# Combining two expert outputs per token: rows of 64 tokens of both choices stacked in the 128 partitions, one matmul in half of the output columns

## The chip, the cores and the metric

One core of one Trainium2 chip runs the whole program. The metric is the device time of one launch in microseconds (us). The kernel before takes 2280.2 us, the median of three runs (2276.58 to 2281.41). All arithmetic is in 32-bit floating point.

## What is computed

The program is one inference step of a decoder layer: RMSNorm, a combined projection, sliding-window attention and a gated delta rule side by side, an output projection, then a mixture of experts in which each token picks two of 64 experts, and a final RMSNorm. It handles 2048 prompt tokens and 64 sample tokens. The change touches only the last step, cut here to what matters:

```python
# hierarchical_moe / reference: two experts per token, gates w0 and w1
y = w0[:, None] * expert_out[first choice] + w1[:, None] * expert_out[second choice]
h = h + y                                  # h: the residual, (tokens, 1024)
out = h * rsqrt(mean(h * h, axis=-1) + 1e-6) * norm_final
```

## The kernel before

The last phase is the function `moe`. Its expert part runs 64 blocks and a few overflow blocks, each with 128 token places: the weights of one expert (3 MB) are loaded by SyncE (SP) into a ring of four buffers in `w_arena`, TensorE (PE) does the three projections (lines 3221 and 3230), and GpSimd (POOL) writes the block's rows to a table `S["y"]` in DRAM with an indirect transfer (line 2911). That table has 2 x 2176 rows of 1024 values: row `t*128 + p` holds the first choice of token p of tile t, the row 2176 further the second choice.

When the last block's rows are in DRAM, ScalarE (ACT) raises `experts_stored`, and the combining stage begins. It runs over 17 tiles: 16 of 128 prompt tokens and one (t = 16) of the 64 sample tokens. `w_arena`, free by now, holds 8 buffers `pair[c]` (two rows of 1024 values a partition, CB = 8) and 8 buffers `out[o]` (OB = 8). Tile by tile:

- **SP**, `fetch(t)`, line 2832: one transfer of 1 MB puts both rows of token p into partition p of `pair[t % 8]`. Eight fetches are issued at the start; `fetch(t + 8)` waits for `weighted` of tile t.
- **ACT**, `weights(t)`, line 3015: two diagonal 128x128 matrices, the identity scaled by the gate of either choice, into `diag`.
- **PE**, `weigh(t)`, line 3260: for each half of the 1024 columns, the first choice's diagonal times the first rows, then the second's added in the same PSUM bank. That is 4 matmuls of 128x512; in 32-bit each is two instructions, so 8 instructions a tile. A tile takes two of the eight PSUM banks, so `weigh(t)` waits for `summed` of tile t - 4.
- **VectorE (DVE)**, `add(t)`, line 3176: PSUM plus the residual `h_all` into `out[t % 8]`. From tile 8 on it waits until the store of tile t - 8 has landed.
- **ACT**, line 3029: the square, with its sum over the row. **POOL**, `root(t)`, lines 2960 and 2962: the power -0.5.
- **DVE**, `scale(t)`, line 3182: the product with the root and the gain. DVE's order is written out: `scale(t - BEHIND)` follows `add(t)`, with BEHIND = 4.
- **SP**, `store(t)`, line 2842: 512 KB to the output. SP's order is written out too: for each t, `fetch(t + 8)`, then `store(t - BEHIND)`.

All of SP's transfers share one queue (q1). Two earlier places of SP are named by the prediction. Line 400 stores the sample tokens' projections from 64 partitions to DRAM; for the table `s_qkv` both sides have 64 rows outermost, and for the table `s_conv_s` the DRAM side is written as 8 sequences x 8 rows, so its outermost dimension has 8 entries while the side in SBUF has 64 partitions. Line 1442 copies caches from DRAM to DRAM; the copies from `in_cache_swa_k` and `in_cache_swa_v` have an outermost dimension of 8 on both sides. Lines 2459 (attention) and 964 (sample projection) are matmuls of 128 rows by 64 output columns that alternate between the output partitions 0 to 63 and 64 to 127.

Of the kernel before, what the change touches and what calls it, by code (L numbers as in the profile page):

```python
# [12 lines left out]
ALU = mybir.AluOpType  # L13
ACT = mybir.ActivationFunctionType
AX = mybir.AxisListType.X

P = 128
D = 1024
# [8 lines left out]
HD = 64  # L27
# [20 lines left out]
HOMES = TILES * P  # L48
# [2611 lines left out]
def moe(nc, A, S, O, K):  # L2660
    T, E = TILES, EPG
# [7 lines left out]
    with Phase(nc, "p5_") as ctx:  # L2669
        sb, sem = ctx.sb, ctx.sem  # L2670
        on = Once(ctx)
# [8 lines left out]
        two = range(2)  # L2680
# [3 lines left out]
        y_arena = sb("y_arena", [P, 6 * DE])  # L2684
        h_all = sb("h_all", [P, T, D])

        def cut(arena, at, shape):
            size = math.prod(shape)
            ap = arena[:, at:at + size]
            if len(shape) == 2:  # L2690
                return ap.rearrange("p (a b) -> p a b", a=shape[0])
            if len(shape) == 3:
                return ap.rearrange("p (a b c) -> p a b c", a=shape[0], b=shape[1])
            return ap
# [6 lines left out]
        y = [cut(y_rows, b * D, (D,)) for b in two]  # L2701
# [2 lines left out]
        midt = [cut(y_arena, (4 + b) * DE, (FC, P)) for b in two]  # L2704

        CB, OB = 8, 8
        BEHIND = 4
        kept = range(BEHIND + 1)
        pair = [cut(w_arena, 2 * c * D, (2, D)) for c in range(CB)]
        ya = [[pair[c][:, k, :] for c in range(CB)] for k in range(2)]  # L2710
        out = [cut(w_arena, (2 * CB + c) * D, (D,)) for c in range(OB)]

        n3 = LAST[1] - LAST[0]
        ident, w = K["ident"], K["w"]
# [28 lines left out]
        spare = sb("spare", [P, 3])  # L2743
        home = [sb(f"home{b}", [P, 1], I32) for b in two]
        gain = cut(y_arena, 0, (D,))
        diag = [[cut(y_arena, D + (2 * b + k) * P, (P,)) for k in range(2)] for b in two]
        half = sb("half", [P, 2 * H])
        ss, ms, rs = ([K["base"][:, at + c:at + c + 1] for c in kept] for at in (NE // 2 + 8, NE // 2 + 16, NE // 2 + 24))
        ps = ctx.psum([P, 8, 512])
# [13 lines left out]
        gathered = [sem(f"gathered{c}") for c in range(CB)]  # L2763
# [12 lines left out]
        def _(sp):  # L2776
# [24 lines left out]
                load_weights(j, j, j % R)  # L2801
            sp.wait_ge(K["ids_out"], 16 * 2 * TILES)
            sp.wait_ge(on["owner_ready"], 1)
            h_flat = h_all[:].rearrange("p t d -> p (t d)")
            with sp.Fori(3 * R, NE - R, R) as i:
                for b in ring:
# [21 lines left out]
            def fetch(t):  # L2828
                r, c = n_rows(t), t % CB
                if t >= CB:  # L2830
                    sp.wait_ge(on["weighted"], t - CB + 1)
                sp.dma_start(pair[c][0:r], S["y"][0:2 * HOMES].rearrange("(k t p) d -> t p k d", k=2, p=P)[t][0:r]
                             ).then_inc(gathered[c], 16)

            for t in two:
                fetch(t)
# [6 lines left out]

            for t in range(T + BEHIND):
                if t + CB < T:
                    fetch(t + CB)
                if t >= BEHIND:
                    store(t - BEHIND)
            for c in range(OB):
# [119 lines left out]
        def _(act):  # L2969
# [40 lines left out]
            def weights(t):  # L3010
                n = t if t < SAMPLES else SAMPLES if t == NT else t + 1
                if t >= 2:
                    act.wait_ge(on["weighted"], t - 1)
                for k in range(2):
                    nc.scalar.activation(diag[t % 2][k], ident[:], ACT.Copy, scale=w[:, n, k:k + 1]).then_inc(on["diag_ready"], 1)

            for t in two:
                weights(t)
            for t in range(T):
                c = t % len(kept)  # L3020
# [7 lines left out]
                r = n_rows(t)  # L3028
# [3 lines left out]
        def _(dve):  # L3032
            own = Chain(dve, on["vec_own"])
            tt, red = nc.vector.tensor_tensor, nc.vector.tensor_reduce
# [57 lines left out]
            step, k = 1, 0  # L3092
            while step < NE:
                own(nc.vector.tensor_copy(cum[1 - k][:, 0:step], cum[k][:, 0:step]))
                own(tt(cum[1 - k][:, step:], cum[k][:, step:], cum[k][:, 0:NE - step], ALU.add))
                step, k = 2 * step, 1 - k
# [28 lines left out]
            def evacuate_y(j, b, sent):  # L3125
                dve.wait_ge(down_done.sem, down_done.part(j, 1))
                dve.wait_ge(y_out[b], sent)
                nc.vector.tensor_copy(y[b][:, 0:512], ps[:, 0 if b else 5, :]).then_inc(y_vec.sem, 1)
# [37 lines left out]
                blocks(i)  # L3166
            blocks(end, 0, 2)
            evacuate_y(end + (R - 1), 1, end * 8 + 8 * R)
            dve.wait_ge(on["h_in"], 16 * (NE // R - 2))

            def add(t):
# [23 lines left out]
        def _(pe):  # L3195
            mm, tr = nc.tensor.matmul, nc.tensor.transpose
# [8 lines left out]
            for n in range(n3):  # L3205
                for k in range(2):
                    t = mm(ps[:, 7, 0:NE], at_lane[:, n, k, :], at_block[:, n, k, :], start=False, stop=(n == n3 - 1 and k == 1))  # L3207
# [3 lines left out]
            for g in range(4):  # L3211
                t = mm(ps[:, 4, g * NE:(g + 1) * NE], sel[:, g].rearrange("p q b -> p (q b)"), token, start=True, stop=True)  # L3212
# [34 lines left out]
            for c in range(FC):  # L3247
                t = tr(ps[:, 7, c * P:(c + 1) * P], mid[1].rearrange("p (f c) -> p c f", c=FC)[:, c], ident[:])
# [3 lines left out]
            def weigh(t):  # L3252
                c, r, at = t % CB, n_rows(t), 2 * (t % 4)
                pe.wait_ge(on["diag_ready"], 2 * t + 2)
                pe.wait_ge(gathered[c], 16 * (t // CB + 1))
                if t >= 4:
                    pe.wait_ge(on["summed"], t - 3)
                for n in two:
                    for k in range(2):
                        ins = mm(ps[0:r, at + n, :], diag[t % 2][k][0:r, 0:r], ya[k][c][0:r, n * 512:(n + 1) * 512],  # L3260
                                 start=(k == 0), stop=(k == 1))
                ins.then_inc(on["weighted"], 1)

            for t in range(T):
# [80 lines left out]
```

## Time and profile before

| | |
|---|---|
| median of three runs | 2280.2 us |
| the profiled execution's own time | 2280.2 us |
| its span, first to last instruction | 2278.4 us |
| PE busy | 2167.0 us, 95% of the span |
| DVE busy | 1287.7 us, 57% |
| ACT / POOL busy | 553.8 us / 591.7 us |
| mean granted TensorE clock | 0.972 |
| the combining stage | from 2198.56 us to the end |

Busy times are of the whole span. The combining stage is its last 80 us, so its limits are read from views cut to that stretch. "SPq" rows are issues of transfers on SP's queue, with the time that the issue took, not the transfer. The DMA share is the mean busy share of 16 DMA engines. The "landing" of a transfer is when its semaphore was raised.

### The profile page before, as it was taken

The numbers are of one execution on the slowest core, as the hardware profiler recorded it, in microseconds if no ns is written. First come the engines' busy times: TensorE is split into PE (matmuls) and PEld (weight loads), VectorE is DVE, ScalarE is ACT, GpSimd is POOL, SyncE is SP. The second block draws the span as 40 slices with busy tenths as digits, with TensorE's granted clock in tenths as the row PEclk, the third lists the DMA queues.
The fourth block names the chain that finished last, engine by engine and source line by source line (L and its number), as shares of the span: only waits on it lengthen the run. The fifth ranks groups of instructions, "written<-read, shape, count | busy, mean of one in ns | idle before, by whom it ended". The sixth has DMA issues, their size and how long they took to land. (4 is left out here: it accounts for less than half of the span.)

```text
span 2278.4 us, 47402 instructions
## 1 busy us (share of the span) xinstructions
PE 2167.0 (95%) x18766; PEld 1175.5 (52%) x18766; DVE 1287.7 (57%) x2657; ACT 553.8 (24%) x1423; POOL 591.7 (26%) x782
## 2 busy tenths in 40 slices
PE   7999999999988899999999999849999999999987
PEld 3444544544545566666666676534444444444433
DVE  4524425323524566566776867357767676767536
ACT  3302202201213344334534444210000000000023
POOL 1110200100200100210032131336555555555522
PEclk9999999999999799999999999959999999999998
DMA  9041040230075522223222221169999999999958
GB/s 324 20 149 34 25 152 28 44 122 13 5 207 155 133 83 80 74 81 105 77 65 91 92 74 38 67 245 340 350 377 365 365 374 376 372 378 365 345 220 315
DMA packets 170897, 405.79 MB, mean 178 GB/s; under 512 B 50195, under 2 KB 91715, under 8 KB 146105
## 3 DMA queue, kind: packets, MB, share of 16 engines
q1 hardware_dynamic: 141559, 349.31, 43.6%
q0 software_dynamic: 22880, 35.11, 4.2%
q10 hardware_dynamic: 6274, 18.72, 2.2%
q8 instruction: 139, 2.28, 0.4%
q14 instruction: 45, 0.37, 0.1%
HBM read 342.85 MB, written 94.80 MB: 192 GB/s over the span
## 5 line engine op out<-in xcount | busy, mean ns | idle before, releaser
L3221 PE MATMUL p_ps<-p_w_arena,k_room 128*128 128x512 f32 x1024 | 452.6, 595 | 13.4 <-DVE k_room L3113 13.4
L3221 PEld LDWEIGHTS p_ps<-p_w_arena,k_room 128*128 128x128 f32 x1024 | 195.2, 191 | 260.5 <-issue 246.5
L2864 POOL DMA_INDIRECT k_room<-s_hn,p_slot x256 | 260.0, 1016 | 123.2 <-issue 63.4
L2478 PE MATMUL p_ps<-k_room,p_mixt 128*128 128x512 f32 x544 | 262.9, 612 | 0.0
L3135 DVE STREAM_TRANSPOSE p_y_arena<-p_y_arena 32x64 f32<-32x64 f32 x1008 | 237.3, 235 | 13.0
L906 PE MATMUL p_ps<-k_room,p_w 128*128 128x512 f32 x544 | 238.9, 594 | 0.0
L906 PE MATMUL p_ps<-p_xt,p_w 128*128 128x512 f32 x544 | 238.1, 593 | 0.5 <-DVE p_xt L725 0.5
L3230 PE MATMUL p_ps<-p_w_arena,p_y_arena 128*128 128x512 f32 x512 | 230.4, 592 | 1.2 <-DVE p_y_arena L3142 0.7
L906 PEld LDWEIGHTS p_ps<-k_room,p_w 128*128 128x128 f32 x544 | 101.4, 190 | 123.0 <-issue 121.0
L906 PEld LDWEIGHTS p_ps<-p_xt,p_w 128*128 128x128 f32 x544 | 101.5, 190 | 122.6 <-issue 120.3
L3230 PEld LDWEIGHTS p_ps<-p_w_arena,p_y_arena 128*128 128x128 f32 x512 | 97.0, 190 | 123.8 <-issue 122.4
L3113 DVE STREAM_TRANSPOSE k_room<-k_room 128x1024 f32<-128x1024 f32 x64 | 129.9, 2030 | 17.1 <-DMA k_room<-s_hn,p_slot 15.3
L2478 PEld LDWEIGHTS p_ps<-k_room,p_mixt 128*128 128x128 f32 x544 | 94.6, 190 | 83.4 <-issue 78.7
L735 DVE TENSOR_SCALAR p_y<-p_ext,p_w_conv 128x512 f32<-128x512 f32 x48 | 23.3, 486 | 193.3 <-ACT p_ext L583 193.3
L2980 ACT ACTIVATE p_y_arena<-p_ps 128x256 f32<-128x256 f32 x64 | 24.6, 384 | 430.1 <-PE p_ps L3221 420.8
L2911 POOL DMA_INDIRECT s_y<-k_room,p_home x66 | 68.5, 1038 | 189.4 <-issue 64.3
L583 ACT COPY p_ext<-p_ps 128x512 f32<-128x512 f32 x48 | 28.1, 586 | 356.7 <-PE p_ps L906 356.7
L739 DVE SCALAR_TENSOR_TENSOR p_y<-p_ext,p_w_conv,p_y 128x512 f32<-128x512 f32 x144 | 108.3, 752 | 5.1
L3119 DVE SCALAR_TENSOR_TENSOR p_y_arena<-p_y_arena,p_ps 128x256 f32<-128x256 f32 x64 | 26.8, 419 | 142.5 <-ACT p_y_arena L2980 137.1
L1521 POOL TENSOR_SCALAR p_ms<-p_ss 128x8 f32<-128x8 f32 x17 | 3.4, 199 | 338.6 <-DVE p_ss L1973 338.6
L2985 ACT COPY k_room<-p_ps 128x512 f32<-128x512 f32 x64 | 37.5, 586 | 204.9 <-PE p_ps L3230 174.0
L526 POOL TENSOR_SCALAR p_ms<-p_ss 128x1 f32<-128x1 f32 (+1 forms) x17 | 6.9, 408 | 296.7 <-ACT p_x L566 196.0
(445 smaller groups left out, 3003.9 us busy)
## 6 DMA issues: line engine op xcount, KB each, us to landing
p_w_arena<-in_w_exp_gate SPq DMA_DIRECT2D x64, 1024.0 KB
p_w_arena<-in_w_exp_up SPq DMA_DIRECT2D x64, 1024.0 KB
p_w_arena<-in_w_exp_down SPq DMA_DIRECT2D x64, 1024.0 KB
p_w_arena<-s_y SPq DMA_DIRECT2D x16, 1024.0 KB, 14.2
p_x<-in_x_prompt SPq DMA_DIRECT2D x30, 512.0 KB, 4.8
s_kv<-p_us SPq DMA_DIRECT2D x32, 256.0 KB
s_kq<-p_y SPq DMA_DIRECT2D x32, 256.0 KB, 2.9
p_kq<-s_kq SPq DMA_DIRECT2D x16, 512.0 KB, 5.9
```

The source lines that it names most:

```text
L583: nc.scalar.copy(ext[q % 3][:, CW - 1:], ps[:, job % 4, :]).then_inc(freed_act.sem, 1)
L739: ins = stt(y[:, c, :], src[:, k:k + SN], w_conv[:, c, k:k + 1], y[:, c, :], ALU.mult, ALU.add)
L906: ins = mm(ps[:, job % 4, :], columns(at, at + P)[:, c], xt[s % 2][:, c, :], start=(c == 0), stop=(c == KC - 1))
L2478: ins = mm(ps[:, 7 - n, :], mixt[t % 2][:, c, :], w_out[:, c, n * 512:(n + 1) * 512], start=(c == 0), stop=(c == KC - 1))
L2864: pool.indirect_dma_start(out=x[b][:, 256 * g:256 * g + 256], out_offset=None, in_=S["hn"].rearrange("t (q k) -> (t q) k", q=4), in_offset ...
L2911: pool.indirect_dma_start(out=S["y"], out_offset=bass.IndirectOffsetOnAxis(ap=home[b][:, 0:1], axis=0), in_=y[b], in_offset=None, bounds_c ...
L2985: nc.scalar.copy(y[b][:, 512:], ps[:, 1 if b else 6, :]).then_inc(y_act.sem, 1)
L3113: nc.vector.transpose(xt[b].rearrange("p c (g r) -> p g c r", g=4), x[bx].rearrange("p (g a c) -> p g c a", g=4, c=KC)).then_inc(xt_ready. ...
L3119: nc.vector.scalar_tensor_tensor(mid[b], th[b], 1.0, ps[:, 2 + b, 0:DE], ALU.add, ALU.mult).then_inc(mid_own.sem, 1)
L3135: t = nc.vector.transpose(midt[b][32 * q:32 * q + 32, :, 32 * g:32 * g + 32], mid[b][32 * g:32 * g + 32].rearrange("p (q a c) -> p q c a", ...
L3221: t = mm(ps[:, 2 + b, :], xt[b][:, c, :], w_gu[bw][:, :, c, :], start=(c == 0), stop=(c == KC - 1))
L3230: t = mm(ps[:, n if b else 5 + n, :], midt[b][:, c, :], w_dn[bw][:, c, n * 512:(n + 1) * 512], start=(c == 0), stop=(c == FC - 1))
```

## The change

`fetch(t)` becomes two transfers of 512 KB. Transfer a (a = 0, 1) takes the tokens 64a to 64a + 63 of the tile and stacks them: the first choice's 64 rows go to partitions 0 to 63, the second choice's to partitions 64 to 127 of `pair[c][:, a]`. The weight matrix `diag[t % 2][:, a]` is now 128x64: `lanes`, two 64x64 identities on top of each other, scaled per partition by the gate that belongs to it. A matmul with it adds both choices at once and writes 64 rows, at partitions 64a of the same PSUM banks. Per tile there are again 4 matmuls (8 instructions) of 512 columns, now in half of the array's columns; the sample tile needs 2. The gates are rearranged for it: SP turns the halves of `w` with two small transfers during the expert part, and DVE adds the identities and copies the gates after `experts_stored`. BEHIND goes from 4 to 2. Line numbers of the changed file are larger by 7 to 16 in this stage.

```diff
-        BEHIND = 4
+        BEHIND = 2
...
-        diag = [[cut(y_arena, D + (2 * b + k) * P, (P,)) for k in range(2)] for b in two]
+        diag = [cut(y_arena, D + 2 * HD * b, (2, HD)) for b in two]
+        lanes = cut(y_arena, D + 4 * HD, (HD,))
+        w_pair = cut(y_arena, D + 5 * HD, (T, 2))
+        w_other = cut(K["base"][:], 0, (T, 2))
...
+            for a in two:
+                sp.dma_start(w_other[a * HD:(a + 1) * HD].rearrange("p t k -> p (t k)"),
+                             w[(1 - a) * HD:(2 - a) * HD].rearrange("p t k -> p (t k)")).then_inc(on["w_turned"], 16)
...
-                sp.dma_start(pair[c][0:r], S["y"][0:2 * HOMES].rearrange("(k t p) d -> t p k d", k=2, p=P)[t][0:r]
-                             ).then_inc(gathered[c], 16)
+                halves = r // HD
+                for a in range(halves):
+                    sp.dma_start(pair[c][:, a], S["y"][0:2 * HOMES].rearrange("(k t a p) d -> t a k p d", k=2, a=2, p=HD)[t, a]
+                                 ).then_inc(gathered[c], 16)
...
-                for k in range(2):
-                    nc.scalar.activation(diag[t % 2][k], ident[:], ACT.Copy, scale=w[:, n, k:k + 1]).then_inc(on["diag_ready"], 1)
+                for a in two:
+                    nc.scalar.activation(diag[t % 2][:, a], lanes, ACT.Copy, scale=w_pair[:, n, a:a + 1]).then_inc(on["diag_ready"], 1)
...
+            act.wait_ge(on["lanes_ready"], 1)
+            act.wait_ge(on["w_paired"], 4)
...
+            dve.wait_ge(on["experts_stored"], 1)
+            tt(lanes, ident[:, 0:HD], ident[:, HD:], ALU.add).then_inc(on["lanes_ready"], 1)
+            dve.wait_ge(on["w_turned"], 32)
+            for k in two:
+                here = slice(k * HD, (k + 1) * HD)
+                nc.vector.tensor_copy(w_pair[here, :, k], w[here, :, k]).then_inc(on["w_paired"], 1)
+                nc.vector.tensor_copy(w_pair[here, :, 1 - k], w_other[here, :, k]).then_inc(on["w_paired"], 1)
...
-                pe.wait_ge(gathered[c], 16 * (t // CB + 1))
+                pe.wait_ge(gathered[c], 32 * (t // CB) + 16 * (r // HD))
...
-                    for k in range(2):
-                        ins = mm(ps[0:r, at + n, :], diag[t % 2][k][0:r, 0:r], ya[k][c][0:r, n * 512:(n + 1) * 512],
-                                 start=(k == 0), stop=(k == 1))
+                    for a in range(r // HD):
+                        ins = mm(ps[a * HD:(a + 1) * HD, at + n, :], diag[t % 2][:, a], pair[c][:, a, n * 512:(n + 1) * 512],
+                                 start=True, stop=True)
```

SP's queue, from the first fetches after the expert part to the end of its stores. Before (`p_w_arena<-s_y` is a fetch, `out_y_prompt<-p_w_arena` a store, `p_y_arena<-in_norm_final` the gain):

```order
L2832 DMA p_w_arena<-s_y 128x2x1024 x2
L2837 DMA p_y_arena<-in_norm_final 128x1024
L2832 DMA p_w_arena<-s_y 128x2x1024 x11
L2842 DMA out_y_prompt<-p_w_arena 128x1024
L2832 DMA p_w_arena<-s_y 128x2x1024
L2842 DMA out_y_prompt<-p_w_arena 128x1024
L2832 DMA p_w_arena<-s_y 128x2x1024
```

With the change, from behind the gain:

```order
L2839 DMA p_w_arena<-s_y 128x1x1024 x18
L2849 DMA out_y_prompt<-p_w_arena 128x1024
L2839 DMA p_w_arena<-s_y 128x1x1024 x2
L2849 DMA out_y_prompt<-p_w_arena 128x1024
L2839 DMA p_w_arena<-s_y 128x1x1024 x2
L2849 DMA out_y_prompt<-p_w_arena 128x1024
L2839 DMA p_w_arena<-s_y 128x1x1024 x2
```

The first store stands behind the fetches of 11 tiles (22 transfers) instead of 13 tiles, and each fetch is two transfers.

DVE, from the last copy of an expert block on. Before:

```order
L3128 COPY k_room<-p_ps 128x512
L3176 TENSOR_TENSOR p_w_arena<-p_ps,p_h_all 128x1024 x5
L3182 SCALAR_TENSOR_TENSOR p_w_arena<-p_w_arena,k_base,p_y_arena 128x1024
L3176 TENSOR_TENSOR p_w_arena<-p_ps,p_h_all 128x1024
```

With the change:

```order
L3137 COPY k_room<-p_ps 128x512
L3179 TENSOR_TENSOR p_y_arena<-k_ident 128x64
L3183 COPY p_y_arena<-k_w 64x17
L3184 COPY p_y_arena<-k_base 64x17
L3183 COPY p_y_arena<-k_w 64x17
L3184 COPY p_y_arena<-k_base 64x17
L3192 TENSOR_TENSOR p_w_arena<-p_ps,p_h_all 128x1024 x3
L3198 SCALAR_TENSOR_TENSOR p_w_arena<-p_w_arena,k_base,p_y_arena 128x1024
L3192 TENSOR_TENSOR p_w_arena<-p_ps,p_h_all 128x1024
```

Five small instructions stand ahead of the first add, and the first scale follows the third add, not the fifth.

## Rows read from the trace of the kernel before

**Rows 1.** The page's chain that ended last, by line.

```profile
PE p_ps L3221 18%; PE p_ps L3230 9%; PE p_ps L3260 3%; DMA p_raw<-s_ids 0%; DMA k_room<-s_hn,p_slot 0%; DMA p_w_arena<-s_y 0%; DVE k_room L3113 0%; POOL k_room L2864 0%; PE p_ps L3207 0%; POOL k_base L2960 0%; DMA s_y<-k_room,p_home 0%; DVE
```

**Rows 2.** The combining stage by stretches; the last three columns: PE clock, DMA share, GB/s.

```profile
2203.50:2221.00 17.50, 17.46 (x37) 7.77 (x38) 4.90 (x4) 6.61 (x15) 2.25 (x6) 0.90 1.02 404
2221.00:2235.00 14.00, 14.00 (x34) 6.14 (x33) 9.17 (x8) 7.65 (x17) 2.96 (x8) 1.00 1.03 410
...
2253.00:2264.00 11.00, 11.00 (x26) 4.03 (x24) 9.12 (x8) 5.77 (x12) 3.06 (x9) 1.00 0.55 224
```

**Rows 3.** Who waited for whom, from 2195 us on: total, times, longest.

```profile
DVE p_w_arena L3176 <- PE p_ps L3260: 30.4, 10, 16.6
...
PE p_ps L3260 <- DMA p_w_arena<-s_y: 10.0, 1, 10.0
DVE p_w_arena L3176 <- DMA out_y_prompt<-p_w_arena: 7.5, 5, 2.4
```

**Rows 4.** Matmul groups by form (array rows * columns, output): busy us, mean ns.

```profile
L3260 PE MATMUL p_ps<-p_w_arena,p_y_arena 128*128 128x512 f32 x128 | 57.0, 608 | 10.0 <-DMA p_w_arena<-s_y 10.0
...
L2459 PE MATMUL p_ps<-p_pt,p_av 128*64 128x512 f32 x128 | 32.6, 632 | 0.0
...
L964 PE MATMUL p_ps<-p_w,p_xt 128*64 128x512 f32 x64 | 14.2, 595 | 0.0
```

**Rows 5.** SP's queue in order of time, the combining stage.

```profile
2198.56 0.89 SPq L2832 DMA_DIRECT2D p_w_arena<-s_y  x2
2199.49 0.47 SPq L2837 DMA_DIRECT2D p_y_arena<-in_norm_final  x1
...
2222.78 0.36 SPq L2832 DMA_DIRECT2D p_w_arena<-s_y  x1
2225.23 0.36 SPq L2842 DMA_DIRECT2D out_y_prompt<-p_w_arena  x1
```

**Rows 6.** DVE in order of time: the ninth add, the last adds, the last scales.

```profile
2237.47 1.22 DVE L3176 TENSOR_TENSOR p_w_arena<-p_ps,p_h_all 128x1024 f32<-128x1024 f32 x1 [1.96 <-DMA out_y_prompt<-p_w_arena]
...
2254.97 1.22 DVE L3176 TENSOR_TENSOR p_w_arena<-p_ps,p_h_all 128x1024 f32<-128x1024 f32 x1
...
2257.30 1.22 DVE L3176 TENSOR_TENSOR p_w_arena<-p_ps,p_h_all 128x1024 f32<-128x1024 f32 x1
...
2264.13 1.22 DVE L3176 TENSOR_TENSOR p_w_arena<-p_ps,p_h_all 64x1024 f32<-64x1024 f32 x1 [1.16 <-PE p_ps L3260]
2265.27 4.85 DVE L3182 SCALAR_TENSOR_TENSOR p_w_arena<-p_w_arena,k_base,p_y_arena 128x1024 f32<-128x1024 f32 x4
2270.83 1.28 DVE L3182 SCALAR_TENSOR_TENSOR p_w_arena<-p_w_arena,k_base,p_y_arena 64x1024 f32<-64x1024 f32 x1 [0.71 <-POOL k_base L2962]
```

**Rows 7.** SP's queue in order of time, the sample tokens' stores (line 400).

```profile
563.29 1.09 SPq L400 DMA_DIRECT2D s_qkv<-p_us  x2
564.42 2.50 SPq L400 DMA_DIRECT2D s_conv_s<-p_us  x4
```

**Rows 8.** Stretches of the line 400 stores; the last two columns: DMA share, GB/s.

```profile
564.50:565.00 0.50, 0.50 (x2) 0.19 (x1) 0.00 (x0) 0.00 (x0) 0.00 (x0) 1.00 0.88 193
...
566.25:567.25 1.00, 1.00 (x4) 0.40 (x3) 0.00 (x0) 0.00 (x0) 0.00 (x0) 1.00 0.48 142
567.25:568.00 0.75, 0.75 (x3) 0.36 (x2) 0.00 (x0) 0.00 (x0) 0.00 (x0) 1.00 0.52 185
```

**Rows 9.** SP's queue in order of time, two of the cache copies (line 1442).

```profile
753.94 0.70 SPq L1442 DMA_DIRECT2D out_k_sample<-in_cache_swa_k  x1
...
756.39 0.67 SPq L1442 DMA_DIRECT2D out_v_sample<-in_cache_swa_v  x1
```

**Rows 10.** Stretches of those copies; the last two columns: DMA share, GB/s of packets begun.

```profile
755.30:756.60 1.30, 0.98 (x57) 0.89 (x58) 0.40 (x1) 0.00 (x0) 0.00 (x0) 0.50 1.24 397
756.60:758.70 2.10, 1.80 (x14) 1.74 (x14) 0.42 (x1) 0.39 (x1) 1.80 (x2) 0.50 0.16 37
758.70:760.20 1.50, 1.50 (x69) 1.10 (x69) 0.69 (x1) 0.20 (x1) 0.35 (x1) 0.50 0.90 352
```

**Rows 11.** ACT and PE in order of time: four diagonals; one tile of line 2459.

```profile
2198.62 1.28 ACT L3015 ACTIVATE p_y_arena<-k_ident,k_w 128x128 f32<-128x128 f32 x4 [4.37 <-DMA s_y<-k_room,p_home]
...
760.07 3.54 PE L2459 MATMUL p_ps<-p_pt,p_av 128*64 128x512 f32 x8
```

More of the change, by code:

```diff
@@ L2706, in moe @@
         CB, OB = 8, 8
-        BEHIND = 4
+        BEHIND = 2
         kept = range(BEHIND + 1)
         pair = [cut(w_arena, 2 * c * D, (2, D)) for c in range(CB)]
-        ya = [[pair[c][:, k, :] for c in range(CB)] for k in range(2)]
         out = [cut(w_arena, (2 * CB + c) * D, (D,)) for c in range(OB)]
```

## The prediction

> **What bounds the kernel now.** I read the chain that ended last first: over the whole span it is expert matmuls, and the changed stage (line 3260) holds 3% of it [rows 1]. All that the change can win lies in the last 80 us. Next the stage cut into stretches [rows 2]: PE is busy through all of it, but the DMA engines are full too, share 1.02 and 1.03 at 404 and 410 GB/s until about 2247 us, and fall to 224 GB/s only after 2253. Then the waits [rows 3]: DVE waited for PE 10 times (30.4 us, of which the first 16.6 are the start) and five times for a store to land (7.5 us). PE waited for data once, at the start. So three things stand close together. PE: 128 instructions in 57.0 us [rows 4], 0.445 each, 3.4 us a tile. DMA: 1 MB in and 0.5 MB out a tile, 1.57 million bytes, 3.84 us at 410 GB/s. DVE: adds 2.33 us apart where nothing holds it (2254.97, 2257.30 [rows 6]).
>
> **A model of the queue.** I take SP's transfers as one line in the order of issue, at 410 GB/s: a fetch 2.56 us, a store or the gain 1.28. Ahead of the first store stand 13 fetches and the gain [rows 5]. The first packets should start near 2200.4 (issue 2198.56, the first tile there at about 2203.5, less 2.56, rounded). Then the store ends at 2200.4 + 13 x 2.56 + 2 x 1.28 = 2236.2. The ninth add, which waits for it, ran at 2237.47 [rows 6]: the model is 1.2 us early, and I add 1.2 us from here on. The same row says that the queue, not the store's own length, makes the 12 us between its issue at 2225.23 and the add.
>
> **The change part by part.**
>
> *The matmuls.* A tile still has 8 instructions, but the two output halves use different columns of the array. Line 964 has this form with both halves alternating: 64 instructions in 14.2 us, 0.222 each; line 2459, 0.255 each [rows 4]. So they run in pairs, 8 x 0.222 = 1.8 us a tile in place of 3.4 at the full clock. At the lower clock, as after an idle stretch, line 2459's eight took 3.54 us [rows 11].
>
> *BEHIND.* The first store stands behind 11 tiles of fetches, not 13. Two scales are left behind the last add instead of four: 4.85 / 2 = 2.4 us less at the end [rows 6].
>
> *Diagonals and gates.* Four ACT instructions took 1.28 us ahead of the first tile [rows 11]; they become smaller but now wait for five small DVE instructions. No such DVE instruction is in the rows; its bounds are nothing and the 1.22 us of a 128x1024 add [rows 6], so five cost at most 6.1 us. I take about 0.2 each, since they handle 17 or 64 elements a partition, 1 us in all. What hides it is the first fetch, 4.9 us from its issue. Without that cover the first tile would start some 2 us late. The two gate transfers of 136 bytes a partition are issued ahead of the weights of expert 12, in front of a full ring; two issues of about 0.5 us as in [rows 5] beside over 3 MB of weights a block: nothing.
>
> *The fetch.* This decides. Before, the fetch had 128 entries outermost on both sides (token p). Now the DRAM side is written (choice, token, value): its outermost dimension has 2 entries, against 128 partitions on the other side. No fetch of that kind is in the trace, so I look for how the engines are shared out. In the stores of line 400, `s_qkv` with 64 rows on both sides filled the engines to 0.88. Then `s_conv_s`, from the same 64 partitions but with 8 outermost entries in DRAM, held the share at 0.48 and 0.52 for 1.75 us [rows 7, 8]: 8 of 16 engines. The 64 partitions did not help; the smaller side counted. Carried over, 2 entries give 2 engines. The two 480 KB cache copies, 8 rows each, show whether another transfer takes other engines. The second was issued at 756.39, yet next to nothing began until 758.7 (37 GB/s), when the first had run out [rows 9, 10]: it queued on the same engines although half of them were free. So I expect all 33 half fetches on the same two engines.
> The price: 262,144 bytes an engine; per engine 410 / 16 = 25.6 GB/s [rows 2], so 10.24 us a half and 20.5 us a tile. From the other side, if the 128 partitions counted, a half costs 1.28 us on 16 engines. I take 10.24, since the 8-against-64 store is the nearest row. If an engine does only what it did there, 185 / 8 = 23.1 GB/s, it is 11.3 us.
> The Trainium skill bears on this (DMA: Bandwidth & Descriptors, section "Why a DMA increments its semaphore by 16 and not by 1"): the number of engines is the largest one up to 16 that divides the slowest dimension of both sides, and they are the lowest-numbered. By that rule the halves get two engines, always the same ones, and the sum is the one below. The row alone would also allow that the written side counts; for this load that is the side with 128, and the sum would be rival A's. No row here shows a count of 2.
>
> *The sum.* On the slowest engine, from 2200.4: 33 halves x 10.24 = 337.9; the gain 1.28; the stores 0 to 6, which all stand ahead of the point that matters, 7 x 1.28 = 9.0. A store still spreads over 16 engines but lines up on these two. The seventh store thus ends at 2548.6, with the 1.2 us at 2549.8. It frees the buffer of the fifteenth add. PE (3.5 us at the low clock against 20.5 a tile), ACT, POOL and DVE are all hidden behind the fetches up to there; the last tile's matmuls begin with the last fetch, one store earlier, and end in time. From the fifteenth add: two add intervals, 4.67 us; from the last add to the scales 1.14, two scales 2.43, POOL's root that DVE's scales hold up 0.71, together 4.28; and from the last scale to the end of the span 2278.4 - 2270.83 = 7.57 [rows 6]. That is 16.5, so the span ends at 2566.3. The profiled execution took 1.8 us more than its span and equals the median of the runs, so I forecast **2568 us**, 288 us slower, 12.6%.
>
> **The rivals.**
>
> *A. The partitions decide, and the halves spread over 16 engines.* For it: a load's far side is DRAM, and the half share was seen at stores. Against it: the smaller side counted there, whichever memory it was in. Then the queue model gives: 11 fetches, gain, first store at 2231.1; five pairs of fetch and store at 3.84, the half fetch of the last tile, and the seventh store: 2231.1 + 19.2 + 1.28 + 1.28 = 2252.9, with 1.2 us 2254.1. PE at 1.8 us no longer holds an add. Plus 16.5 the span ends at 2270.6, the time is 2272.4: 7.8 us or 0.34% **faster**, which is this change ending on the other side. It holds from the point at which the halves use enough engines for 3.84 us a tile, all 16.
>
> *B. As A, but the half-column matmuls run one after the other.* PE stays at 3.4 us a tile, the last add at 2264.13, and only the two scales are won: 2277.8. Against it are the 0.222 us of line 964.
>
> *C. Two engines a half, but others each time.* With up to eight tiles in flight the queue would again use all engines, and it ends like A. Against it is the second cache copy.
>
> *D. Two engines, but slower than a full set each.* At 23.1 GB/s an engine: halves 11.35 x 33 = 374.5, stores and gain 8 x 1.42 = 11.4, so 38.9 more: 2607. At the 142 / 8 = 17.8 GB/s of the other stretch it would be above 2700, but that stretch had gaps between issues of 0.6 us.
>
> **How the numbers follow.** Two fixed engines, 0.85 (with D's slower rates 0.12 of these); A and C 0.11; B and a wide fetch with a new small loss 0.04, split between no change and slower. A measurement of this kernel can tell about 0.2%, 4.6 us, from no change. So faster 0.11, same 0.03, slower 0.86. The likeliest case's range: below, the line without its seven stores (9 us less) and at a rate as far above 410 as that is above 404, 1.5% (5 us), with a margin for the model; above, D with a margin for two busy engines that lose time between transfers: 2545 to 2632. That leaves out A, B and C and a little of D, under 2 in 10.
>
> **What would show it.** Right: about 20.5 us between tiles at line 3276; a DMA share near 0.13 and 51 GB/s or a little more with the stores; PE waiting for the fetch 16 times; the median landing of a half fetch beyond 50 us or SP's issues stalled; 128*64 matmuls at the low clock. Wrong, in A's sense: DMA share at 1.0 through the stage, landings of some 15 us, 0.22 us a matmul, and DVE waiting for stores. If the share is 0.25 or 0.5, the rule for the number of engines is another.

## The result, and the profile after

| | before | after |
|---|---|---|
| time of the runs, median (range) | 2279.7 us (2276.6 to 2281.4), 4 runs | 2565.3 us (2563.7 to 2567.9), 4 runs |
| profiled execution: time, span | 2280.2, 2278.4 us | 2563.8, 2561.8 us |
| mean granted PE clock | 0.972 | 0.917 |
| first fetch issued | 2198.56 us | 2198.55 us |
| from there to the end of the span | 79.8 us | 363.3 us |

The change makes the kernel slower: ratio 1.1253, 95% interval 1.1234 to 1.1272. The forecast was 2568 us with a range of 2545 to 2632. The fetches start at the same moment in both profiled executions, so all of the 283 us between their spans lies in the last stage.

The chain that ended last, from the page, in place of [rows 1]:

```profile
PE p_ps L3237 16%; PE p_ps L3246 8%; DMA out_y_prompt<-p_w_arena 5%; SPq L2839 2%; DMA p_w_arena<-s_y 1%; PE p_ps L3276 1%; SPq L2844 1%; DMA s_y<-k_room,p_home 1%; DMA p_raw<-s_ids 0%; SPq L2849 0%; POOL k_room L2871 0%; DVE p_w_arena L3192 0%; DVE p_w_arena L3198 0%; POOL k_base L2967 0%; DVE p_y_arena L3144 0%
```

Before, the stage's part of it was matmuls (line 3260, 3%). Now it is stores that wait in the queue (5%), SP that cannot issue its fetches (L2839) and the gain (L2844), and the fetches themselves. Two stretches close to the first two of [rows 2], and three later ones. The columns are the stretch, its length, the busy time of PE, of its weight loads, of DVE, ACT and POOL, and last the granted PE clock, the DMA share and GB/s:

```profile
2205.00:2221.00 16.00, 0.00 (x0) 0.00 (x0) 0.00 (x0) 0.00 (x0) 0.00 (x0) 0.50 0.13 52
2221.00:2235.00 14.00, 3.62 (x8) 0.85 (x8) 1.22 (x1) 1.73 (x4) 0.00 (x0) 0.62 0.25 82
2300.00:2400.00 100.00, 17.67 (x40) 4.30 (x40) 9.66 (x8) 7.54 (x18) 2.96 (x8) 0.59 0.13 52
2400.00:2500.00 100.00, 18.25 (x40) 4.25 (x40) 9.66 (x8) 6.52 (x16) 2.97 (x8) 0.53 0.18 75
2500.00:2540.00 40.00, 7.36 (x16) 1.72 (x16) 4.84 (x4) 3.26 (x8) 1.48 (x4) 0.54 0.33 133
```

A share of 0.13 is 2 of 16 engines, at 52 GB/s where there were 404. They are not slow engines: 52 / 2 = 26 GB/s each, against 404 / 16 = 25. From 2400 us on stores, which use all engines, are mixed in, and share and rate rise. A clock of 0.50 to 0.62 means that PE is most of the time at the lower of its two levels, 1.2 GHz; it had been idle for 16 us or more before each full tile. PE in order of time:

```profile
2221.59 3.62 PE L3276 MATMUL p_ps<-p_w_arena,p_y_arena 128*64 128x512 f32 x8 [28.04 <-DMA p_w_arena<-s_y]
2242.41 3.45 PE L3276 MATMUL p_ps<-p_w_arena,p_y_arena 128*64 128x512 f32 x8 [17.20 <-DMA p_w_arena<-s_y]
2263.74 3.68 PE L3276 MATMUL p_ps<-p_w_arena,p_y_arena 128*64 128x512 f32 x8 [17.88 <-DMA p_w_arena<-s_y]
2283.82 3.68 PE L3276 MATMUL p_ps<-p_w_arena,p_y_arena 128*64 128x512 f32 x8 [16.39 <-DMA p_w_arena<-s_y]
2303.84 3.46 PE L3276 MATMUL p_ps<-p_w_arena,p_y_arena 128*64 128x512 f32 x8 [16.34 <-issue]
```

From 2263.74 to 2303.84 there are two tiles in 40.1 us: 20.05 a tile, 10.03 a half. Most of PE's waits are put down to "issue" though the tile is as late as the others. The waits from 2195 us on (total, times, longest), against [rows 3]:

```profile
PE p_ps L3276 <- issue: 211.9, 13, 17.8
...
DVE p_w_arena L3192 <- DMA out_y_prompt<-p_w_arena: 158.6, 7, 55.3
DVE p_w_arena L3192 <- PE p_ps L3276: 154.7, 8, 26.1
...
PE p_ps L3276 <- DMA p_w_arena<-s_y: 79.5, 4, 28.0
```

PE waits 211.9 + 79.5 = 291.4 us in 17 stretches, once for each tile, because the half fetches come 10 us apart. "Issue" is where the trace names no releaser. DVE waited for stores before too, but never longer than 2.4 us; now one such wait is 55.3 us. SP's queue in order of time, against [rows 5], and DVE around that wait:

```profile
2198.55 12.94 SPq L2839 DMA_DIRECT2D p_w_arena<-s_y  x4
2211.53 16.79 SPq L2844 DMA_DIRECT2D p_y_arena<-in_norm_final  x1
2228.37 172.99 SPq L2839 DMA_DIRECT2D p_w_arena<-s_y  x18
2401.41 9.81 SPq L2849 DMA_DIRECT2D out_y_prompt<-p_w_arena  x1
2411.26 10.97 SPq L2839 DMA_DIRECT2D p_w_arena<-s_y  x2
```

```profile
2268.60 1.28 DVE L3198 SCALAR_TENSOR_TENSOR p_w_arena<-p_w_arena,k_base,p_y_arena 128x1024 f32<-128x1024 f32 x1
...
2426.22 1.22 DVE L3192 TENSOR_TENSOR p_w_arena<-p_ps,p_h_all 128x1024 f32<-128x1024 f32 x1 [55.33 <-DMA out_y_prompt<-p_w_arena]
...
2447.52 1.23 DVE L3192 TENSOR_TENSOR p_w_arena<-p_ps,p_h_all 128x1024 f32<-128x1024 f32 x1 [18.89 <-DMA out_y_prompt<-p_w_arena]
...
2543.94 1.23 DVE L3192 TENSOR_TENSOR p_w_arena<-p_ps,p_h_all 128x1024 f32<-128x1024 f32 x1 [8.83 <-DMA out_y_prompt<-p_w_arena]
...
2548.60 1.21 DVE L3192 TENSOR_TENSOR p_w_arena<-p_ps,p_h_all 64x1024 f32<-64x1024 f32 x1
...
2551.72 1.28 DVE L3198 SCALAR_TENSOR_TENSOR p_w_arena<-p_w_arena,k_base,p_y_arena 128x1024 f32<-128x1024 f32 x1 [0.72 <-POOL k_base L2969]
2553.71 1.27 DVE L3198 SCALAR_TENSOR_TENSOR p_w_arena<-p_w_arena,k_base,p_y_arena 64x1024 f32<-64x1024 f32 x1 [0.71 <-POOL k_base L2969]
```

SP is stuck in its own issues: eighteen fetches in 173 us, some 9.6 each, where one had taken 0.36 to 0.45 us [rows 5]. That is close to the 10 us that a half fetch takes, so SP issues only as fast as the two engines work off what is queued. The first store's tile was scaled at 2268.60, but 22 half fetches stand ahead of the store in SP's program, so it is issued at 2401.41. The ninth add waits for it until 2426.22. The next five adds follow 21.3 us apart, two halves and a store.

### The profile page after: what moved, and what is told of

Its sections match the earlier page's. It is cut to its first block and busy times, and to the rows that moved or that the text cites. A ratio compares the mean times of both kernels' runs of the same rounds, so it can differ in the third digit from the quotient of the medians.

```text
span 2561.8 us, 47421 instructions
## 1 busy us (share of the span) xinstructions
PE 2169.4 (85%) x18762; PEld 1166.6 (46%) x18762; DVE 1289.1 (50%) x2662; ACT 552.0 (22%) x1423; POOL 590.4 (23%) x782
## 5 line engine op out<-in xcount | busy, mean ns | idle before, releaser
L3276 PE MATMUL p_ps<-p_w_arena,p_y_arena 128*64 128x512 f32 x132 | 61.2, 1052 | 291.4 <-issue 211.9
L3192 DVE TENSOR_TENSOR p_w_arena<-p_ps,p_h_all 128x1024 f32<-128x1024 f32 (+1 forms) x17 | 20.8, 1223 | 313.3 <-DMA out_y_prompt<-p_w_arena 158.6
L3276 PEld LDWEIGHTS p_ps<-p_w_arena,p_y_arena 128*64 128x64 f32 x132 | 14.4, 217 | 337.5 <-issue 337.5
## 6 DMA issues: line engine op xcount, KB each, us to landing
p_w_arena<-in_w_exp_gate SPq DMA_DIRECT2D x64, 1024.0 KB, 13.3
```

The source lines that it names most:

```text
L3276: ins = mm(ps[a * HD:(a + 1) * HD, at + n, :], diag[t % 2][:, a], pair[c][:, a, n * 512:(n + 1) * 512], start=True, stop=True)
```

## The experiments

Stages of different profiled executions are compared by one number that each trace gives: from the issue of the first fetch to the end of the span (before 79.8, after 363.3 us). The first issue moves between executions with the expert stage ahead of it, from 2193.2 to 2206.1 us in the traces of this case, so a span alone is a poor measure of 5 us.

### Is the whole loss the transfer's form?

**The old matmuls with the new fetches.** In the kernel before, line 2832 (the sample tile keeps its one transfer, which is not shown):

```diff
-sp.dma_start(pair[c][0:r], S["y"]... "(k t p) d -> t p k d" ...[t][0:r]).then_inc(gathered[c], 16)
+for a in range(2):
+    sp.dma_start(pair[c][:, a], S["y"]... "(k t a p) d -> t a k p d" ...[t, a]).then_inc(gathered[c], 16)
```

> The kernel before with the fetches of the 16 full tiles written as the change writes them (two transfers a tile, 2 entries outermost in DRAM against 128 partitions), and nothing else of the change; full matmuls, BEHIND = 4. The rows thus lie stacked where the matmuls expect them side by side, so the combination mixes other rows than the reference. Theory: 32 halves at 10.0 us, a stage of 360 us: 2550 to 2572 us, DMA share 0.13. Rival (it takes the new matmuls or the wait on two transfers to be slow): about 2280 us.

Measured: 2563.4 us (one run), the stage 361.5. The weighing in halves, the diagonals, the gates' transfers and the number of scales left behind are all as before here, and the time is that of the change. So the form of the transfer is enough for the loss, and no other part of the change is needed. It is not the same stage to the microsecond: it has 32 narrow halves and not 33, which is 10 us less, yet it is only 1.8 us shorter. The other 8 us are not separated; in this run the first store stands behind 13 tiles, and the last three adds each wait about a microsecond for the full matmuls.

### Would a wider form repair it?

**Two transfers a tile, cut by choice, 64 entries outermost on both sides.** Choice k goes to partitions 64k to 64k + 63. The matmuls and the data are those of the change.

```diff
-for a in range(halves):
-    sp.dma_start(pair[c][:, a], S["y"]... "(k t a p) d -> t a k p d" ...[t, a])
+for k in two:
+    sp.dma_start(pair[c][k * HD:(k + 1) * HD, 0:halves], S["y"]... "(k t a p) d -> k t p a d" ...[k, t][:, 0:halves])
```

> The changed kernel with one edit: the two transfers of a tile are cut by choice instead of by 64 tokens, so that both sides have 64 entries outermost (64 partitions; token rows), 512 KB each as before; everything else of the change stays, and the data that arrive are the same. Theory (the outermost dimension of 2 confined each fetch to two engines): the stage is limited by all 16 engines again, 3.84 us a tile; 2272 us, 7 to 8 us below the kernel before; DMA share 1.0 until about 2250 us, 0.22 us a matmul. Rival (stacking in 128 partitions is itself slow, or the half-column matmuls or the low clock cost the time): stays above 2500 us. Rival (all that is left is BEHIND): 2277 to 2278 us.

**The same with BEHIND = 4.**

> As the run with the transfers cut by choice, with BEHIND back at 4. Theory: the first store stands behind 13 fetches again and two more scales follow the last add; no add waits for PE any more. By the queue model the ninth add runs at 2237.5, the thirteenth at 2251.4 and the last some 10 us later, 2275.5 us in all, 3 us above the version with 2 and 4 to 5 us below the kernel before. Rival (BEHIND matters nothing once PE is fast): equal to that version, 2272 us.

Measured: 2314.7 us (ratio 1.0138, 1.0121 to 1.0156), stage 110.1; with BEHIND = 4 2317.2 us (1.0163, 1.0149 to 1.0176), stage 115.0. That is 2.5 us more at the median, with intervals that overlap. Both expectations were missed, by 43 and 42 us: the fix took away 250 us of the loss and left the kernel slower than before. Its stretch of 2220 to 2240 us, columns as above:

```profile
2220.00:2240.00 20.00, 11.60 (x32) 2.99 (x32) 7.25 (x6) 6.14 (x14) 2.95 (x8) 0.70 1.04 213
```

All 16 engines are busy and yet move half of what they did: 13.3 GB/s each. So there is a second cost, which the share of busy time hides. All 16 engines are in use in this form; what else is new is where the bytes land, 64 partitions a transfer, and that is tried below.

**BEHIND = 2 in the kernel before.**

```diff
-        BEHIND = 4
+        BEHIND = 2
```

> The kernel before with BEHIND = 2 alone. Theory: PE at 3.4 us a tile still sets the last add at 2264.1 us, so only the two scales behind it are won, 2.4 us: 2277.5 us. Rival (the stores are what holds it, and earlier stores help as much as the fast matmuls): 2272 to 2274 us. Rival (the root comes too late for a scale two tiles behind): 2280 us or more.

Measured: 2280.8 us beside 2281.0 of the kernel before, ratio 1.000 (0.999 to 1.001); stage 78.2, 1.6 us less than before. The time alone fits the third expectation, but the root is not late: it holds up one scale, the last, by 0.7 us as before. The last rows of DVE do what the prediction took from [rows 6]: the last scale begins 4.3 us after the last add where it had been 6.7.

```profile
2264.33 1.22 DVE L3176 TENSOR_TENSOR p_w_arena<-p_ps,p_h_all 64x1024 f32<-64x1024 f32 x1 [1.16 <-PE p_ps L3260]
...
2268.64 1.28 DVE L3182 SCALAR_TENSOR_TENSOR p_w_arena<-p_w_arena,k_base,p_y_arena 64x1024 f32<-64x1024 f32 x1 [0.71 <-POOL k_base L2962]
```

No add waits for a store any more, but all 17 wait for PE, so earlier stores did not make the last add earlier. The 2.4 us at the end are seen in the trace and are too little to show in twelve runs, whose interval is 2 us to either side.

### How the engines are shared out

**4, 8, 16 and 128 entries outermost.** The changed kernel, each half fetch taken from so many equally long blocks of rows; shown for 4, the others put 8 or 16 in its place, and the last one takes 128 rows in sequence. All four fetch other rows than the tokens need; only their times are of use.

```diff
-sp.dma_start(pair[c][:, a], S["y"][0:2 * HOMES]... "(k t a p) d -> t a k p d" ...[t, a])
+at = (2 * t + a) % 16 * (P // 4)
+sp.dma_start(pair[c][:, a], S["y"][0:SEQ].rearrange("(q r) d -> q r d", q=4)[:, at:at + P // 4])
```

> The changed kernel with the DRAM side of each half fetch written as 4 blocks of 32 rows, the blocks 512 rows apart, against the same 128 partitions; 512 KB as before. It fetches other rows of the table than the reference needs. Theory (engines = largest number up to 16 that divides both outermost counts, always the same ones): 4 engines, 5.0 us a half, 10.0 us a tile; 33 x 5.0 and 10 us of stores and gain after 2200.4, then 19: 2395 to 2400 us, DMA share 0.25. Rival (2 engines for anything that is not one block): 2565 us. Rival (others each time): near 2272 us.

> The same with 8 blocks of 16 rows, 256 rows apart; other rows than the reference needs. Theory: 8 engines, 2.5 us a half, 5.0 us a tile; 2312 to 2318 us, DMA share 0.5 in the stretch of fetches. Rival (others each time, so that transfers in flight fill all 16): 2272 us.

> The same with 16 blocks of 8 rows, 128 rows apart; other rows than the reference needs. Theory: 16 engines, 1.25 us a half; 2271 to 2274 us, as with the transfers cut by choice, DMA share 1.0. Rival (scattered blocks or 128 partitions cost rate by themselves): above 2280 us.

> The changed kernel with each half fetch taking 128 consecutive rows of the table, so that both sides have 128 entries outermost and each of the 16 engines writes its own 4-partition groups; other rows than the reference needs. This is the change without its narrow transfers. Theory (two costs add up: few engines, and, in the run cut by choice, 16 engines that all write into 64 partitions at 213 GB/s): full rate, 410 GB/s, and the queue model of rival A: 2272 us, 7 to 9 us below the kernel before. Rival (something else in the change costs as well): 2280 us or more.

| entries outermost | time, us | stage, us | DMA share | GB/s |
|---|---|---|---|---|
| 2 (the change) | 2565.3 | 363.3 | 0.13 | 52 |
| 4 | 2396.4 | 198.3 | 0.26 | 105 |
| 8 | 2318.2 | 116.8 | 0.51 | 208 |
| 16 | 2289.6 | 94.5 | 1.03 | 261 |
| 128 | 2272.3 | 73.6 | 1.02 | 416 |

Those with 4, 8 and 16 entries are one run each. The first two came out as expected, 2396.4 of 2395 to 2400 and 2318.2 of 2312 to 2318. Share and GB/s are of the stretch of 2220 to 2240 us, here with 4, 8, 16 and 128 entries (for 2 of the long middle above):

```profile
2220.00:2240.00 20.00, 7.36 (x16) 1.72 (x16) 3.64 (x3) 3.47 (x8) 2.24 (x6) 0.50 0.26 105
```

```profile
2220.00:2240.00 20.00, 11.62 (x32) 2.98 (x32) 7.25 (x6) 5.63 (x14) 2.95 (x8) 0.67 0.51 208
```

```profile
2220.00:2240.00 20.00, 12.12 (x42) 3.20 (x40) 9.66 (x8) 7.54 (x18) 3.69 (x10) 0.84 1.03 261
```

```profile
2220.00:2240.00 20.00, 13.97 (x52) 3.82 (x54) 11.47 (x10) 8.37 (x20) 3.83 (x11) 0.91 1.02 416
```

Up to 8 the share is the number of entries over 16, at 26 GB/s an engine. The rule that the prediction weighed (the Trainium skill, DMA: Bandwidth & Descriptors, section "Why a DMA increments its semaphore by 16 and not by 1") gives the same counts, and the trace agrees for 2, 4 and 8. With 16 blocks of 8 rows the expectation of 2271 to 2274 was missed by 16 us: all engines are busy, at 16 GB/s each. With 128 single rows the stage runs at 416 GB/s and the time is 2272.3 us, ratio 0.9968 (0.9958 to 0.9979). That is the case of the prediction's rival A (all engines at full rate) and its 2272.4 us. It also shows the reverse of the first experiment: with all else of the change in place, the loss is gone once the fetch has another form.

In that run PE has what the change was to give it. A tile of eight matmuls takes 1.94 us at the full clock, 0.24 each, where [rows 4] had 0.445:

```profile
2225.08 1.94 PE L3276 MATMUL p_ps<-p_w_arena,p_y_arena 128*64 128x512 f32 x8 [0.62 <-ACT p_y_arena L3022]
```

### Where the bytes land

**Each choice on partitions of both halves of the memory.** As the wide form, but choice 0 to partitions 32 to 95, and choice 1 in two transfers to 0 to 31 and 96 to 127.

```diff
-    sp.dma_start(pair[c][k * HD:(k + 1) * HD, 0:halves], ...[k, t][:, 0:halves])
+y_rows_of = S["y"]... "(k t a p) d -> k t p a d" ...
+sp.dma_start(pair[c][32:96, 0:halves], y_rows_of[0, t][:, 0:halves])
+for n in two:
+    sp.dma_start(pair[c][96 * n:96 * n + 32, 0:halves], y_rows_of[1, t][32 * n:32 * n + 32, 0:halves])
```

> As the run cut by choice, but the first choice's 64 rows go to partitions 32 to 95 in one transfer and the second's to 0 to 31 and 96 to 127 in two; the matmuls are unchanged, so the combination mixes other rows than the reference. Theory (the destination's partitions decide: 0 to 63 reach half of the write paths, 32 to 95 all of them, 32 partitions half): half of the bytes at 410 and half at 210 GB/s, 278 GB/s on average, 3.8 us a tile in the first stretch instead of 4.9; the end at 2290 to 2298 us. Rival (64 partitions are slow wherever they lie): 2315 us, 213 GB/s. Rival (three transfers a tile cost more issue time on SP): above 2315 us.

**The wide form on two queues.** Choice 0 by SP as before, choice 1 (partitions 64 to 127) issued by ACT, so that both can be under way at once.

```diff
+def fetch_second(t):
+    act.dma_start(pair[c][HD:P, 0:halves], ...[1, t][:, 0:halves]).then_inc(gathered[c], 16)
```

> As the run cut by choice, with the second choice's transfers issued by ACT on its own queue, so that transfers to partitions 0 to 63 and to 64 to 127 are in flight side by side. The data are the reference's. Theory (only the write paths of one half at a time limit the rate, and an engine with two queues alternates between the halves): 330 to 410 GB/s in the first stretch, 2272 to 2280 us, at or a little below the kernel before. Rival (two transfers are never fused, each runs at half the rate): 213 GB/s, 2315 us. Rival (ACT's issues delay diagonals and squares): DVE waits for ACT and POOL, some us above 2280.

Measured: 2290.0 us (one run, stage 94.1) and 2294.6 us (ratio 1.0072, 1.0058 to 1.0086, stage 92.3), against the wide form's 2314.7 and 110.1. The stretches of 2220 to 2240 us, first the run with 32 to 95, then the one with two queues:

```profile
2220.00:2240.00 20.00, 11.79 (x40) 3.14 (x40) 7.96 (x7) 6.50 (x16) 2.95 (x8) 0.83 1.03 265
```

```profile
2220.00:2240.00 20.00, 11.63 (x46) 3.12 (x42) 12.78 (x11) 8.75 (x21) 3.69 (x10) 0.96 1.03 290
```

The first changes nothing but the partitions and, with them, the cut of choice 1, and its stage is 16 us shorter: the destination is a limit by itself. Stretches of one microsecond between the gain and the first store, where only fetches run, show both kinds in turn:

```profile
2214.00:2215.00 1.00, 0.69 (x4) 0.00 (x0) 0.80 (x2) 0.79 (x4) 0.32 (x2) 1.00 0.93 209
2216.00:2217.00 1.00, 0.68 (x4) 0.40 (x6) 1.00 (x1) 1.00 (x2) 0.00 (x0) 1.00 1.00 397
2218.00:2219.00 1.00, 0.26 (x2) 0.00 (x0) 0.71 (x1) 0.59 (x2) 0.04 (x1) 1.00 1.00 221
```

Between 2208 and 2220 us the rate rises to 307 to 397 GB/s about once in 3.8 us, the time of a tile, and lies at some 210 to 250 in between. That fits the order of the transfers, one to 32 to 95 and two to 32 partitions each; the trace does not name the transfer in a stretch. The Trainium skill has such a limit (SBUF — State Buffer, section "Door 1: The DMA port swizzle (why `[64,N]` ≈ `[32,N]`)"): partitions 0 to 63 reach only half of the ports, 32 to 95 all of them. The trace agrees on the direction and on the size of the wide form (213 of 410 GB/s), and the time, 2290.0 us, lies at the lower edge of what was expected of a mix of both kinds (its first issue came early, at 2193.9 us, which helped). The second run fell between theory and rival. Two half-width transfers on two queues overlap in part, at 290 GB/s, and do not add up to full rate. That ACT issued too late is not the reason: the DMA share is 1.03, and a fetch of either queue landed 24 us after its issue at the median, so both queues always held work.

### Versions that beat both

**The change with the rows interleaved.** Partition 2p + k holds choice k's row of token p. The far side has 64 entries outermost, the near side all 128 partitions.

```diff
-sp.dma_start(pair[c][:, a], S["y"]... "(k t a p) d -> t a k p d" ...[t, a])
+sp.dma_start(pair[c][:, a], S["y"]... "(k t a p) d -> t a p k d" ...[t, a])
-tt(lanes, ident[:, 0:HD], ident[:, HD:], ALU.add)
+cols = ident[:].rearrange("q (p k) -> q p k", k=2)
+tt(lanes, cols[:, :, 0], cols[:, :, 1], ALU.add)
+nc.vector.tensor_reduce(odd, cols[:, :, 1], AX, ALU.add)
...
+tt(w_step, w_both[:, :, :, 1], w_both[:, :, :, 0], ALU.subtract)
+nc.vector.scalar_tensor_tensor(w_pair..., w_step, odd, w_both[:, :, :, 0], ALU.mult, ALU.add)
```

> The changed kernel with the halves' rows stacked alternately instead of one choice above the other: partition 2p+k holds choice k's row of token p, so the DRAM side is written (token, choice, value) with 64 entries outermost against 128 partitions. Weights, diagonals and the row sums follow that order and all is computed. Theory: both costs are gone, since 64 and 128 share 16 engines and one transfer covers all partitions; then the stage is the queue's at 404 to 420 GB/s and the time is rival A's, 2270 to 2275 us. Rival 1: an engine takes four neighbouring tokens, so eight neighbouring partitions, as in the run with 16 blocks of 8 rows: about 256 GB/s, 2287 to 2293 us. Rival 2: the written side's shape (128 single rows) doesn't help and the 64 outermost entries behave as the 64-partition transfers did: 213 GB/s, 2310 to 2318 us.

**The kernel before, three tiles without PE.** BEHIND = 2, and DVE alone combines tiles 9, 11 and 13.

```diff
+if t in (9, 11, 13):
+    dve.wait_ge(gathered[c], 16 * (t // CB + 1))
+    scalar_tensor_tensor(ya[0][c], ya[0][c], w[:, n, 0:1], h_all[:, t, :], ALU.mult, ALU.add)
+    ...
+    scalar_tensor_tensor(out[o], ya[1][c], w[:, n, 1:2], ya[0][c], ALU.mult, ALU.add)
+    return
```

> The kernel before with BEHIND = 2 and tiles 9, 11 and 13 combined on DVE alone (two scalar_tensor_tensor of 128x1024 a tile, no matmuls, no diagonals), everything computed. Theory: the kernel before has two bounds close together at the end, PE (last add 2264.3) and the transfers; with 14 instead of 17 tiles PE ends 3 x 3.4 = 10 us earlier, DVE has 3 x 1.3 = 4 us more to do with 1.1 us free a tile, and the queue sets the last stores: 2271 to 2276 us. Rival 1: DVE becomes the bound with the longer tiles near the end: 2277 to 2283 us. Rival 2: the run of BEHIND = 2 alone showed no gain because the transfers already set the end, and taking work from PE gives nothing: 2278 to 2281 us.

| | time, us | before in the same batch | ratio | first issue to end |
|---|---|---|---|---|
| interleaved | 2278.3 (12 runs) | 2282.8 (23 runs) | 0.9977 (0.9966 to 0.9988) | 74.2 us |
| three tiles on DVE | 2276.2 (12 runs) | 2282.8 | 0.9968 (0.9957 to 0.9980) | 73.9 us |

Both are faster than before, by 0.2 and 0.3%, with intervals that leave out 1. Neither absolute range decides much, since the kernel before ran 3 us longer in this batch; the stages do. The interleaved version in its stretch of 2220 to 2240 us:

```profile
2220.00:2240.00 20.00, 15.03 (x64) 4.41 (x62) 14.50 (x12) 11.02 (x26) 4.92 (x13) 1.00 1.03 411
```

The full rate is back, so both rivals (about 256 and 213 GB/s) are out. The stage is 79.8 - 74.2 = 5.6 us shorter, against 7.8 by rival A's sum. Its first issue came at 2206.10, which is the reason why this profiled execution has a span of 2280.3.

With three tiles on DVE the stage is 5.9 us shorter, of which BEHIND = 2 alone had given 1.6. It did not come as it was reasoned. DVE in order of time:

```profile
2239.97 1.23 DVE L3195 TENSOR_TENSOR p_w_arena<-p_ps,p_h_all 128x1024 f32<-128x1024 f32 x1 [1.02 <-PE p_ps L3281]
2241.11 1.28 DVE L3201 SCALAR_TENSOR_TENSOR p_w_arena<-p_w_arena,k_base,p_y_arena 128x1024 f32<-128x1024 f32 x1
2242.30 1.28 DVE L3185 SCALAR_TENSOR_TENSOR p_w_arena<-p_w_arena,k_w,p_h_all 128x1024 f32<-128x1024 f32 x1
2243.62 1.28 DVE L3189 SCALAR_TENSOR_TENSOR p_w_arena<-p_w_arena,k_w 128x1024 f32<-128x1024 f32 x1
2244.82 1.28 DVE L3201 SCALAR_TENSOR_TENSOR p_w_arena<-p_w_arena,k_base,p_y_arena 128x1024 f32<-128x1024 f32 x1
...
2263.51 1.22 DVE L3195 TENSOR_TENSOR p_w_arena<-p_ps,p_h_all 64x1024 f32<-64x1024 f32 x1 [0.68 <-PE p_ps L3281]
```

It waits about a microsecond for PE at each add up to 2239.97, and from 2242.30 on it works without a gap until shortly before the last add. So rival 1's mechanism came true, DVE became the bound near the end, though the stage still gained by it: the last add came 62.0 us after the first issue (2263.51 - 2201.48), where before it was 65.6.

## Why the prediction was right

The time was met to 3 us, and so was the way to it: 20.05 us between tiles, a DMA share of 0.13 at 52 GB/s, 17 waits of PE, SP stalled in its issues. That the sum came so close is in part luck, since two of its errors run against each other.

**Two engines for a half fetch.** Right, and always the same ones, or the eight tiles in flight would have used more. The step was carried over from one store with 8 entries against 64 partitions [rows 7, 8]; the series 2, 4, 8 confirms it for loads.

**The price of a half.** Forecast 10.24 us, measured 10.03: 33 x 0.21 = 6.9 us too much. The 404 and 410 GB/s of [rows 2] make 25.3 and 25.6 an engine; in this stage one moved 262,144 bytes in 10.03 us, 26.1.

**Where the line ends.** The seventh store was to free the fifteenth add at 2549.8; the add ran at 2543.94, 5.9 us earlier, which is the term above less a microsecond. That it is the seventh store and not the last fetch was right: the row names the store as its releaser.

**The end.** 16.5 us from the fifteenth add, measured 2561.8 - 2543.94 = 17.9. The two add intervals are right (4.66 against 4.67). POOL's root held DVE up twice, not once (0.72 and 0.71), and from the last scale to the end it is 8.1 us, not 7.57. The two errors, a point reached 5.9 us earlier and an end 1.4 us longer, left 2561.8 against 2566.3.

**SP.** Stalled issues were named as a sign but not priced. They delayed the first store from 2269.9, when it was ready, to 2401.41 and made the longest wait of DVE, 55.3 us. By the prediction's own sum it cost no time, since the same two engines have the same bytes to move in any order (no run of this form had its stores issued earlier); the term "the stores ahead of the point that matters, 7 x 1.28" holds wherever they stand.

**Matmuls, diagonals, gates.** 3.45 to 3.68 us a tile at the low clock against 3.54 from [rows 11]; 1.94 at the full clock where 1.8 was taken. (3.4 us a tile for the full form is not 8 x 0.445, which is 3.56, but the distance of SP's stores in the trace of before, 2225.23, 2228.66, 2232.10; the forecast of 2568 us does not use it.) The five small DVE instructions took 0.16 to 0.23 us each beside the first fetch:

```profile
2198.55 0.23 DVE L3179 TENSOR_TENSOR p_y_arena<-k_ident 128x64 f32<-128x64 f32 x1 [5.99 <-ACTq L3015]
2198.70 0.16 DVE L3183 COPY p_y_arena<-k_w 64x17 f32<-64x17 f32 x1
```

They were done by 2199.3, and the first tile began at 2221.59, released by its fetch, so nothing of them showed.

**The rivals.** A, the queue at full rate, gave 2272.4 us, and the run with 128 entries gave 2272.3. As an account of what limits a fetch it was too simple, though: it put the point "all 16 engines", and the wide form and the one of 16 blocks had all 16 and did not reach it. B fell with the 1.94 us a tile in that run. C and D fell with the share of 0.13 and the 26 GB/s. D's sum has a slip: 374.5 + 11.4 less 348.2 is 37.7 us, not 38.9, so 2606 us; it changes neither the range nor a chance.

**Open.** Why 16 blocks of 8 rows run at 261 GB/s with all engines busy. Neighbouring partitions for each engine were suspected. But the blocks also lie 128 rows apart in DRAM, and no run separates the two. Neither is enough by itself: if an engine takes whole blocks, then with 4 and 8 blocks it wrote 32 and 16 neighbouring partitions, from blocks 512 and 256 rows apart, and kept its 26 GB/s; only with all 16 engines at work did each fall to 16. The interleaved version shows only that 64 entries of 2 rows are free of it. Nor was it tried to spread the DVE tiles over the stage, or to combine them with the interleaved fetch.

## What to carry to other kernels

When a transfer is rewritten so that a small dimension (a choice, a half, a head) comes first on either side, count its outermost entries: here the same bytes made the stage 4.5 times as long (363 against 80 us). Where the order in the partitions is free, as it is when a matrix sums over them, put the small dimension innermost: (token, choice) in place of (choice, token) was a change of two letters in the transfer and of the constants around it, and turned 12.5% slower into 0.2% faster. Where 64 partitions are all that a transfer covers, it also matters which: see the rates below. And read GB/s beside the DMA share, because a share of 1.0 stood beside 213, 261 and 416 GB/s.

## What the hardware showed that I had not expected

- Transfers to 64 partitions (0 to 63 or 64 to 127) kept all engines busy at 213 GB/s, half of the 404 to 416 of those to 128; to 32 to 95 and the rest, in turn, 265, with single microseconds at 397 and at 209; the first kind on two queues at once, 290.
- 16 blocks of 8 rows moved 261 GB/s with all engines busy (16 each), where 8 blocks of 16 rows on half of the engines moved 208 (26 each).
- With two engines to a transfer an issue of SP took some 10 us (17 for the gain) and not 0.4, so a store that was ready waited 131 us behind the fetches ahead of it.
